# Merging blocks of a gated recurrence by products of gates, instead of by exponentials of differences of log sums

## The reference

```python
G = jnp.cumsum(log_f, axis=1)
decay = jnp.where(causal, jnp.exp(jnp.minimum(G[:, :, None] - G[:, None, :], 0.0)), 0.0)
A = jnp.einsum('bihk,bjhk,bijhk->bhij', q, k, decay)
o = jnp.einsum('bhij,bjhv->bihv', A, v) + jnp.einsum('bihk,bhkv->bihv', q * jnp.exp(G), S)
k_dec = k * jnp.exp(G_last[:, None] - G)
S_new = jnp.exp(G_last)[..., None] * S + jnp.einsum('bjhk,bjhv->bhkv', k_dec, v)
```

## Time and profile before

| | |
|---|---|
| median of 3 runs | 3410.09 us (3404.29 to 3411.52) |
| span of the profiled execution, which is its time here | 3414.2 us |
| busy over the span: PE, DVE, ACT, POOL | 91%, 55%, 31%, 13% |
| the recurrence: from its first instruction to its last gate product | 1264.3 to 1646.6 us |
| PE clock over the span, mean granted | 0.943 of 2.4 GHz |

### The profile page before, as it was taken

One profiled execution on the slowest core, in us unless ns is written; L12 is line 12 of the kernel. 1 busy time (PEld: TensorE's weight loads), 2 busy tenths in 40 slices (PEclk: granted clock), 3 DMA queues, 4 the chain that ended last, 5 costly groups with the idle time before them and its releaser, 6 DMA issues.

```text
span 3414.2 us, 43368 instructions
## 1 busy us (share of the span) xinstructions
PE 3117.2 (91%) x17124; PEld 2740.5 (80%) x17124; DVE 1866.3 (55%) x2445; ACT 1057.1 (31%) x1661; POOL 427.9 (13%) x594
## 2 busy tenths in 40 slices
PE   6999999978997977676689999998999999999999
PEld 5887779867886875666589999987999998788887
DVE  5322532148896869999444454553445444455554
ACT  3122312124553654444221222221322221232221
POOL 2200220001000017787100000000000000000000
PEclk9999999979997987878899999999999999999999
DMA  4333233121102221222321212232222121332221
GB/s 171 112 114 120 99 112 119 56 70 36 31 18 58 69 81 45 72 75 59 130 99 50 74 51 74 75 109 79 71 74 72 52 75 50 127 109 77 75 89 49
DMA packets 205465, 271.27 MB, mean 79 GB/s; under 512 B 46984, under 2 KB 146764, under 8 KB 205264
## 3 DMA queue, kind: packets, MB, share of 16 engines
q1 hardware_dynamic: 205264, 268.50, 23.7%
HBM read 211.43 MB, written 57.03 MB: 79 GB/s over the span
## 4 chain that ended last, share of the span: by engine, by line
PE 49%; DMA 1%; DVE 1%; ACT 1%; issue 0%; SPq 0%; POOL 0%; POOLq 0%; ACTq 0%
PE mf_psO L1681 27%; PE mf_psT L1719 22%; DMA mf_nat<-scratch_mix 1%; PE mf_psT L1667 1%; DVE mf_wlo L1568 0%; ACT mf_whi L1498 0%; DVE mf_hs L1597 0%; DVE mf_acc L1591 0%; ACT mf_hs L1522 0%; ACT mf_xhi L1513 0%; DVE mf_xlo L1581 0%; DVE mf_acc L1638 0%; POOL mf_rstd L1489 0%; SPq L1443 0%; SPq L1474 0%
## 5 line engine op out<-in xcount | busy, mean ns | idle before, releaser
L1638 DVE TENSOR_TENSOR mf_acc<-mf_psO,mf_acc 128x1024 f32<-128x1024 f32 x272 | 332.9, 1224 | 383.8 <-PE mf_psO L1681 383.8
L1719 PE MATMUL mf_psT<-mf_xhi,mf_whi 128*128 128x384 f32 (+1 forms) x1536 | 493.3, 321 | 15.3 <-issue 9.9
L1719 PE MATMUL mf_psT<-mf_xlo,mf_whi 128*128 128x384 f32 (+1 forms) x1536 | 492.9, 321 | 0.0
L1719 PE MATMUL mf_psT<-mf_xhi,mf_wlo 128*128 128x384 f32 (+1 forms) x1536 | 492.7, 321 | 0.0
L1681 PE MATMUL mf_psO<-mf_whi,mf_uhi 128*128 128x512 f32 (+1 forms) x1088 | 426.4, 392 | 0.0
L1681 PE MATMUL mf_psO<-mf_whi,mf_ulo 128*128 128x512 f32 (+1 forms) x1088 | 425.5, 391 | 0.0
L1681 PE MATMUL mf_psO<-mf_wlo,mf_uhi 128*128 128x512 f32 (+1 forms) x1088 | 425.3, 391 | 0.0
L1498 ACT ACTIVATE mf_whi<-mf_st 128x2048 fp32r<-128x2048 f32 x108 | 201.8, 1909 | 640.0 <-PE mf_psO L1681 613.9
L1719 PEld LDWEIGHTS mf_psT<-mf_xhi,mf_whi 128*128 128x128 f32 x1536 | 291.0, 189 | 18.9 <-issue 16.1
L1719 PEld LDWEIGHTS mf_psT<-mf_xlo,mf_whi 128*128 128x128 f32 x1536 | 291.0, 189 | 1.8
L1719 PEld LDWEIGHTS mf_psT<-mf_xhi,mf_wlo 128*128 128x128 f32 x1536 | 291.0, 189 | 0.0
(11 more groups left out here) (191 smaller groups left out, 5418.3 us busy)
## 6 DMA issues: line engine op xcount, KB each, us to landing
mf_st<-in_w_up SPq DMA_DIRECT2D x48, 1024.0 KB, 6.2
mf_st<-in_w_down SPq DMA_DIRECT2D x48, 1024.0 KB, 5.0
pj_wst<-in_w_in SPq DMA_DIRECT2D x28, 1024.0 KB, 7.0
scratch_proj<-pj_ob SPq DMA_DIRECT2D x80, 256.0 KB, 2.0
mf_st<-in_w_o SPq DMA_DIRECT2D x12, 1024.0 KB, 6.1
pj_xin<-in_x_prompt SPq DMA_DIRECT2D x16, 512.0 KB, 3.9
mf_nat<-scratch_mix SPq DMA_DIRECT2D x16, 512.0 KB, 5.8
mf_xin<-in_x_prompt SPq DMA_DIRECT2D x16, 512.0 KB, 3.7
```

Source lines behind the costliest of these rows:

```text
L1638: nc.vector.tensor_tensor(acc[0:r, i, :], psO[k % 2][0:r, :], acc[0:r, i, :], ALU.add).then_inc(s["o_out"], 1)
L1719: last = nc.tensor.matmul(ps, wa[b4][:, w0:w0 + P], xa[:, j, c0:c0 + cn], start=j == 0 and q == 0, stop=j == KD - 1 and q == 2)
```

## The change

Nothing is logarithm or exponential any more. The running sum and its differences go, and with them the clamps, `keep`, `rc_gs`, `rc_d`, `rc_e` and `rc_x`. In their place a tile keeps two arrays that are updated in place and a small one:

- `rc_qp` starts as q times f (POOL, L1073), and in block size m holds q times the product of the gates from the start of the block to the row
- `rc_k` itself, which in block size m holds k times the product of the gates behind the row to the end of the block
- `rc_tot`, the product of all gates of a block, half as many numbers at each level (256, 128, ..., 4)

Levels now go upward, from blocks of 1 to blocks of 64. Product i of a tile reads `rc_k` and `rc_qp` (L1234). When it is done, the merge i multiplies the upper halves of `rc_qp` by the total of the lower half (DVE, L1149, 128x256), the lower halves of `rc_k` by the total of the upper half (POOL, L1084, 128x256), and the two totals into one (DVE, L1151). Product i+1 waits for both. So the levels of a tile are a chain, where they were independent of each other before. After the last merge `rc_k` and `rc_qp` are the decayed keys and queries that the transposes (L1244) and the output product (L1272) need.

A tile starts every NPOS = 9 spots, and its eight products stand two spots apart, so that the products of two tiles alternate. `take` stays on DVE for the diagonal and the five smaller levels (L1163); levels 6 and 7 are copied by ACT as whole blocks, in three instructions a tile. The product by g moves from DVE to POOL (L1100).

```diff
-        NPOS = 8
-        EXP, MULT, PROD, TAKE = 1, 2, 3, 4
-        FRONT_A, LN, FRONT_B, FRONT_C, D2, E12 = 1, 3, 4, 5, 3, 8
-        QK, KHT, KHN, SPROD, SOUT, OPROD, SQ, RMS, RS, OSC, GATE = 9, 10, 11, 12, 13, 13, 14, 15, 17, 18, 19
+        NPOS = 9
+        TAKE = 1
+        KHT, KHN, SPROD, SOUT, OPROD, SQ, RMS, RS, OSC, GATE = 16, 17, 18, 19, 17, 18, 19, 20, 21, 22
+        prods = {NPOS * n + 2 * i: (n, i) for n in range(N) for i in range(levels(n) + 1)}
...
 (POOL)
-                    pool.wait_ge(s["e_ready"], u + 1)
...
-                    nc.gpsimd.tensor_tensor(xv[:, :, 0:m], ev[:, :, 0:m], blk(k[n % NL], n, m)[:, :, 0:m], ALU.mult)
-                    nc.gpsimd.tensor_tensor(xv[:, :, m:2 * m], ev[:, :, m:2 * m],
-                                            blk(q[n % NL], n, m)[:, :, m:2 * m], ALU.mult).then_inc(s["x_ready"], 1)
+                n = tile_at(spot, 0)
+                if n is not None:
+                    wait_loaded(pool, n)
+                    if n >= NQ:
+                        pool.wait_ge(s["o_done"], n - NQ + 1)
+                    nc.gpsimd.tensor_tensor(flat(qp[n % NQ], n), flat(q[n % NL], n), flat(f[n % NL], n),
+                                            ALU.mult).then_inc(s["qp_begun"], 1)
+                if prods.get(spot - TAKE, (0, 0))[1]:
...
+                    pool.wait_ge(s["a_ready"], prod_no[n, i] + 1)
+                    if i >= 2:
+                        pool.wait_ge(s["tot_ready"], merge_no[n, i - 1] + 1)
...
+                    nc.gpsimd.tensor_tensor(kv[:, :, 0:m], kv[:, :, 0:m],
+                                            halves(n, m)[:, :, 1:2].to_broadcast([P, nb, m]),
+                                            ALU.mult).then_inc(s["ks_ready"], 1)
...
+                n = tile_at(spot, GATE)
+                    pool.wait_ge(s["osc_ready"], n + 1)
+                    nc.gpsimd.tensor_tensor(on[bb][0:r, :], on[bb][0:r, :], g[n % NL][0:r, :],
+                                            ALU.mult).then_inc(s["on_ready"], 1)
...
 (DVE)
+            def merge(n, i):
...
+                dve.wait_ge(s["a_ready"], prod_no[n, i] + 1)
...
+                    dve.wait_ge(s["tot_ready"], merge_no[n, i - 1] + 1)
+                qv, hv = pairs(qp[n % NQ], n, m), halves(n, m)
+                nc.vector.tensor_tensor(qv[:, :, m:2 * m], qv[:, :, m:2 * m],
+                                        hv[:, :, 0:1].to_broadcast([P, nb, m]), ALU.mult).then_inc(s["qp_ready"], 1)
+                nc.vector.tensor_tensor(totals(n, 2 * m).rearrange("p (b t) -> p b t", t=1), hv[:, :, 0:1],
+                                        hv[:, :, 1:2], ALU.mult).then_inc(s["tot_ready"], 1)
...
+            for spot in SPOTS:
+                z = prods.get(spot - TAKE)
+                if z and z[1]:
+                    merge(*z)
+                if z in dve_no:
+                    take(*z)
...
 (PE)
+                    if i == 0:
+                        wait_loaded(pe, n)
+                    elif i == 1:
+                        pe.wait_ge(s["qp_begun"], n + 1)
+                    else:
+                        pe.wait_ge(s["qp_ready"], merge_no[n, i - 1] + 1)
+                        pe.wait_ge(s["ks_ready"], merge_no[n, i - 1] + 1)
```

More of the change, by code:

```diff
@@ L933, in recur, with ring @@
         masks = S.sb("rc_masks", [P, 8, P])
-        keep = {r: S.sb(f"rc_keep{r}", [P, H * r]) for r in (P, NEW)}
         minus_half = S.sb("rc_mhalf", [P, H])
[L937 to L948, removed]
+        def ring(name, n, w=W):
+            return [S.sb(f"rc_{name}{i}", [P, w]) for i in range(n)]
+        NL, NQ = 4, 3
+        q, f, k, v, g = (ring(z, NL) for z in ("q", "f", "k", "v", "g"))
+        qp, tot = ring("qp", NQ), ring("tot", NQ)
+        khn, sqo, on = (ring(z, 2) for z in ("khn", "sqo", "on"))
+        so, rs = ring("so", 2, H), ring("rs", 2, H)
+        At = [S.sb(f"rc_At{n}", [P, H, P]) for n in range(3)]
         St = [S.sb(f"rc_S{i}", [P, H, P]) for i in range(3)]
@@ L963, in levels @@
         def levels(n):
[L964 to L973, removed]
-        NPOS = 8
-        EXP, MULT, PROD, TAKE = 1, 2, 3, 4
-        FRONT_A, LN, FRONT_B, FRONT_C, D2, E12 = 1, 3, 4, 5, 3, 8
-        QK, KHT, KHN, SPROD, SOUT, OPROD, SQ, RMS, RS, OSC, GATE = 9, 10, 11, 12, 13, 13, 14, 15, 17, 18, 19
-        SPOTS = range((N - 1) * NPOS + GATE + 1)
+            return tiles[n][1].bit_length() - 1
+        NPOS = 9
+        TAKE = 1
+        KHT, KHN, SPROD, SOUT, OPROD, SQ, RMS, RS, OSC, GATE = 16, 17, 18, 19, 17, 18, 19, 20, 21, 22
+        SPOTS = range((N - 1) * NPOS + GATE + 1)
+        prods = {NPOS * n + 2 * i: (n, i) for n in range(N) for i in range(levels(n) + 1)}
+        order = [prods[z] for z in sorted(prods)]
+        prod_no = {z: p for p, z in enumerate(order)}
+        merges = [z for z in order if z[1]]
+        merge_no = {z: p for p, z in enumerate(merges)}
+        by_act = [z for z in order if z[1] >= 6]
+        by_dve = [z for z in order if z[1] < 6]
+        act_no = {z: p for p, z in enumerate(by_act)}
+        dve_no = {z: p for p, z in enumerate(by_dve)}
         def tile_at(spot, step):
@@ L986, in tile_at, with wait_taken @@
             return n if i == 0 and 0 <= n < N else None
[L988 to L996, removed]
         def wait_loaded(eng, n):
             eng.wait_ge(loaded[n % NL], 16 * 5 * (n // NL + 1))
+        def wait_taken(eng, z):
+            if z in act_no:
+                eng.wait_ge(s["placed"], act_no[z] + 1)
+            else:
+                eng.wait_ge(s["taken"], dve_no[z] + 1)
         def at(n):
@@ L1008, in heads, with pairs, totals, halves @@
             return flat(buf, n).rearrange("p (h t) -> p h t", h=H)
-        def blk(buf, n, m):
+        def pairs(buf, n, m):
             return flat(buf, n).rearrange("p (b t) -> p b t", t=2 * m)
+        def totals(n, m):
+            c = H * tiles[n][1]
+            if m == 1:
+                return f[n % NL][:, 0:c]
+            return tot[n % NQ][:, c - 2 * c // m:c - c // m]
+        def halves(n, m):
+            return totals(n, m).rearrange("p (b t) -> p b t", t=2)
         block = ctx.enter_context(nc.Block())
@@ L1049, in _ @@
             for i in range(3):
-                nc.gpsimd.memset(At[i][:, :, :], 0.0)
-            for r in (P, NEW):
-                last = nc.gpsimd.memset(keep[r][:, :], 1.0)
+                last = nc.gpsimd.memset(At[i][:, :, :], 0.0)
             last.then_inc(s["maskstep"], 1)
@@ L1071, in _ @@
                     pool.wait_ge(s["maskstep"], step)
-                    nc.gpsimd.affine_select(out=mv, in_=mv, compare_op=ALU.is_ge, fill=0.0, base=base,
-                                            pattern=[[-2 * m * mult, P // (2 * m)], [0, 2 * m]],
-                                            channel_multiplier=mult).then_inc(s["maskstep"], 1)
+                    last = nc.gpsimd.affine_select(out=mv, in_=mv, compare_op=ALU.is_ge, fill=0.0, base=base,
+                                                   pattern=[[-2 * m * mult, P // (2 * m)], [0, 2 * m]],
+                                                   channel_multiplier=mult)
@@ L1113, in _ @@
         @block.scalar
         def _(act):
[L1115 to L1121, removed]
-            for spot in SPOTS:
[L1123 to L1132, removed]
+            act.wait_ge(s["init"], 1)
@@ new lines, in _ @@
+            for spot in SPOTS:
+                if prods.get(spot - TAKE) in act_no:
+                    n, i = prods[spot - TAKE]
+                    m, p = 1 << (i - 1), prod_no[n, i]
+                    act.wait_ge(s["a_ready"], p + 1)
+                    act.wait_ge(s["taken"], dve_no[n, 5] + 1)
+                    for b in range(0, P, 2 * m):
+                        last = nc.scalar.activation(at(n)[b:b + m, :, b + m:b + 2 * m],
+                                                    psA[p % NA][b:b + m, :, b + m:b + 2 * m], ACT.Copy)
+                    last.then_inc(s["placed"], 1)
@@ L1211, in state_out @@
                         dve.wait_ge(s["state_loaded"], 16)
+                    dve.wait_ge(s["tot_ready"], merge_no[n, levels(n)] + 1)
+                    whole = totals(n, tiles[n][1])
                     for h in range(H):
                         last = nc.vector.scalar_tensor_tensor(
-                            out=new[:, h, :], in0=old[:, h, :], scalar=heads(e1[bb], n)[:, h, tiles[n][1] - 1:tiles[n][1]],
+                            out=new[:, h, :], in0=old[:, h, :], scalar=whole[:, h:h + 1],
                             in1=psS[:, h, :], op0=ALU.mult, op1=ALU.add)
@@ L1272, in _ @@
+            for spot in SPOTS:
+                z = prods.get(spot - TAKE)
[3 more added lines that the diff above has]
+                    take(*z)
+                for step, do in ((SOUT, state_out), (RMS, out_rms), (OSC, out_scale)):
                     n = tile_at(spot, step)
-                    if n is not None and n + ahead < N:
-                        do(n + ahead)
```

(11 more changed lines are left out.)

130 lines of the change are left out of this document (28 added, 102 removed).

## The result

The changed kernel takes 3290.22 us (3286.35 to 3299.27, four runs) against 3410.81 for the one before (3404.29 to 3415.05, four runs): a ratio of 0.9645, 95% interval 0.9625 to 0.9665. It is 121 us faster, where 80 were forecast; by the ratio it lies at 3289 on the forecast's scale, just under the range's lower end of 3290.

The account below looks back on a forecast made before the run. DVE was taken to bound the recurrence. Masks to 1274.7, small tile 5, 16 periods of 16.7 (267) and tail 20 end at 1567, 80 us less: 3334 as a span, 3330 as median, range 3290 to 3370.

Parts of the forecast that it names:

- What bounds the kernel now: Recurrence before the change: DVE sets the pace, busy 96% of 371.0 us, a tile every 21.80 us.
- What two instructions cost side by side: Merges: DVE's two-input product waits for POOL's to end, so a pair starting together costs 1.2 us, not 0.85.
- The prices: Instruction costs in the changed stage: PE product 0.89 us, POOL broadcast product 0.85 to 0.91, root pair 1.37, state update 1.02 to 1.09.
- A period walked through: Older tile W, newer X, V ahead of W, from W's product 4 to X's: 15.9 us a tile at full clock.
- chain of X behind the gate of V: POOL's queue in a period: X2's keys, ready at 9.0, stand behind V's gate product, which ends at 11.0.
- The clock: PE's clock in the stage: 0.90, one fifth of the time low, making the period 16.7 us.
- The sum: Whole stage: masks to 1274.7, small tile 5, 16 periods 267, tail 20, end at 1567, 80 us less.
- the tail: After the last tile's product 4, through output products, root pair and product by g: 17.6 us, 20 with some low clock.
- the first (ports free of each other, 13.9, 3285): DVE and POOL do not block each other, or seldom meet, at full clock: 125 us less; chance 15%.
- The slower rivals: Clock as before, 3345 to 3370, 22%; chain slower than DVE's old work, 3437, 4%; no measurable change, 3400, 3%.
- the second rival: PE's clock in the stage stays as before: period 17.6 us, 3345, to 3370 with more waits; chance 22%.
- What would show it: Profile signs: period 15 to 17.5 us, DVE near 80%, L1149 mean near 0.7, POOL waiting before L1100, clock 0.85 to 0.95.

Follow-up runs that it names:

- b3: The kernel before, with only the copies of its two largest levels moved to ScalarE: 3385.4 us, ratio 0.9932.
- b1: The kernel before, with only the copies of its two largest levels moved to ScalarE and the product by g to GpSimd: 3404.8 us, ratio 0.9972.
- e5: The changed kernel with the product by g on GpSimd at spot 27 in place of 22: 3277.4 us, ratio 0.9612.
- e1: The changed kernel with the product by g back on VectorE: 3281.6 us, ratio 0.9618.
- e2: The changed kernel with all eight masked copies on VectorE, none on ScalarE: 3327.4 us, ratio 0.9756.
- e8: The changed kernel with GATE = 27, GpSimd's root pair two spots later, VectorE's scaling behind it, and totals after the masked copy: 3276.3 us, ratio 0.9606.
- e10: The changed kernel with GATE = 27 and VectorE's total of a merge behind the masked copy: 3274.9 us, ratio 0.9604.

## Why the prediction was right and wrong

- **What bounds the kernel now**: right. Shown by b3 (less VectorE, less time at once) and by b1 (less VectorE, given back in longer VectorE instructions beside GpSimd's).
- **What two instructions cost side by side**: that VectorE's product waits for GpSimd's held, with 1.23 in place of 0.16. GpSimd's waits as well. Who waits was wrong. I priced the two halves of a merge at 1.2 us together, and named a mean near 0.7 for L1149. It is 433 ns. Where both start together, VectorE's half is first by a few hundredths, GpSimd's is done 0.9 to 1.0 after that instead of 1.2, and VectorE's wait falls on the small totals.
- **The prices**: the broadcast product on GpSimd is 0.62 alone, not 0.85: cheaper than its upper and lower ends, which came from products of two full arrays. PE's prices, the copies, the update and the root pair fit to 0.1.
- **A period walked through**: the step that failed. To VectorE's merge of X1 it ran within 0.4 us of the trace (t = 0 at 1400.4, rc_qp of X1 at 6.3 to 6.6 against 6.7 to 7.0). Then it let the 256-wide total of X1 wait for GpSimd's keys, 1.2 us, when they start after it (1406.99 and 1407.15). In the trace that total takes 0.42. So scaling, gate product and X2's keys came 1.2 to 1.7 us late; the two merges behind them, at 1.2 instead of 1.0, add the rest of 1.8, and the period was 15.9 instead of 14.1. The chain of X behind the gate of V is there (e5, e1), at 0.65 us a tile.
- **The clock**: forecast at 0.90 for the 16 periods, measured at 0.94 (1280.3 to 1513.4), and at 1.00 from 1316 to 1520; for the whole stage it is 0.92. The low level cost 7.2 us over 16 periods (233.1 - 16 x 14.12), where 12.8 were forecast (16 x 0.8). At low clock throughout the walk said 21; one tile of the start took 22.3 at a clock of 0.67.
- **The sum**: the starts of VectorE's merges behind product 4 give its terms, in the small tile, the first three full tiles and the last:

```profile
1280.28 0.56 DVE L1149 TENSOR_TENSOR rc_qp<-rc_qp,rc_tot 128x64 f32<-128x64 f32 x1 [0.51 <-PE rc_psA L1234]
...
1294.50 0.42 DVE L1149 TENSOR_TENSOR rc_qp<-rc_qp,rc_tot 128x256 f32<-128x256 f32 x1 [1.46 <-PE rc_psA L1234]
...
1316.80 0.43 DVE L1149 TENSOR_TENSOR rc_qp<-rc_qp,rc_tot 128x256 f32<-128x256 f32 x1 [0.77 <-PE rc_psA L1234]
...
1329.83 0.42 DVE L1149 TENSOR_TENSOR rc_qp<-rc_qp,rc_tot 128x256 f32<-128x256 f32 x1 [0.53 <-PE rc_psA L1234]
...
1513.35 0.43 DVE L1149 TENSOR_TENSOR rc_qp<-rc_qp,rc_tot 128x256 f32<-128x256 f32 x1 [0.54 <-PE rc_psA L1234]
```

The 16 periods took 233.1 us, where 267 were forecast. The start (4.7 us against 5) and the tail (20.6 against 20) fit, and the masks ended 0.9 later than forecast. So the 33 us by which the stage ended earlier than forecast are the term of the period: 28 by the walk (16 x 1.8) and 6 by the clock, less 1 elsewhere. Of the 121 us in the times, 80 were forecast, these are 33, 4 lie behind the stage, and 4 are the difference between the profiled executions and the medians. The mechanism held in the main, the term of the period was mis-sized.
- **The rivals**: the first (ports free of each other, 13.9, 3285) named the nearest time and period by luck, for a reason that does not hold: VectorE and GpSimd do hold each other up, 1.1 us in one total. The slower rivals did not come; e2, with a period of 17.14 against the second rival's 17.6, shows how near that is when two copies more stand on VectorE.
- **What would show it**: VectorE's share (79%) and the stage's clock (0.92) were right, and so was that PE's L1234 waits for L1084 more than for L1149, though the profile's names say the opposite. Wrong were the period of 15 to 17.5 us (14.12), the mean of L1149, and the wait of POOL ahead of L1100: it waited 0.8 us for DVE's L1200 in the sum over 16 tiles.

What stays open: why the period is 14.1 and not 13.4 to 13.9 in terms of one bound. No engine is full (PE 80%, DVE 87% in the middle), and no plain theory told all the runs. How far the low clock at the start is the same in every execution was not tried. In the profile of the change it lasted 41 us (10.9 of them before PE's first product) and then 3.4, in those of e8 and e10 20.5 and then 3.4; so the spans of single profiles can't be compared to a few us, the periods can.

## What to carry to other kernels

A step that is replaced by cheaper ones on the fullest engine pays until the engines' queues interlock; from there on, what counts is what stands ahead of the newest tile's next step, and two copies of 0.7 us at the wrong place cost 3.0 us a tile (e2), 1.6 of them through the clock. When two tiles are interleaved, give the newer one the way. Where two engines hold each other up, put the long two-input instructions of one where the other has none, before moving any work: moving the 128x512 product by five spots gained 13 us, moving the 128x256 ones to the faster engine cost 33. And where an engine waits for two semaphores, compare the ends of both producers before believing the releaser that the profile names.

## What the runs showed of the hardware

- A two-input product of 8 elements a partition on VectorE took 1.23 us beside GpSimd's 128x512 product (the change), and 0.16 alone (e5). It ended when the other engine's instruction did (1410.12 and 1410.09).
- A GpSimd product with a broadcast operand, written in place, took 0.62 us, and 0.85 with two full ones into a third array, for the same 128x256; which of the two differences counts was not tried. With VectorE's product just ahead of it, it took 0.87 to 0.99.
- TensorE's clock was at the high level for 204 us (the change, 1316 to 1520), with waits of PE of at most 1.0 us in the regular periods. In e2, with a wait of 2.0 us in each period, it fell to the low level in ten periods and stayed up in others with the same wait; a period with a fall was 1.6 us longer.
